# Two tiles of block two's first output projection as a pair with two groups of seven block products, and ScalarE's loop over pooled groups written out

## The reference, cut to what matters

```
hdn = rmsnorm(x, norm_a);  u, gate = hdn @ w_in_a          # two halves of 2048
z[:, g] = (pool_g(u[:, g]) @ w_grp_a[g]) * scale_a[g]      # g = 0..3, windows 2, 4, 8, 16
y = (z * silu(gate)) @ w_out_a;  x = x + y                 # "first output projection"
kv_in = rmsnorm(x, norm_kv);  k = rope(kv_in @ w_k);  v = kv_in @ w_v
```

## Time and profile before

| | us |
|---|---|
| median of 3 runs | 2318.03 (2317.78 to 2319.93) |
| profiled execution, its own time | 2317.87 |
| its span | 2316.1 |
| PE busy | 2299.1 (99%) |
| DVE busy | 1824.8 (79%) |
| ACT busy | 1185.2 (51%) |
| POOL busy | 449.1 (19%) |

### The profile page before, as it was taken

One profiled execution on the slowest core, in us unless ns is written; L12 is line 12 of the kernel. 1 busy time (PEld: TensorE's weight loads), 2 busy tenths in 40 slices (PEclk: granted clock), 3 DMA queues, 4 the chain that ended last, 5 costly groups with the idle time before them and its releaser, 6 DMA issues.

```text
span 2316.1 us, 31102 instructions
## 1 busy us (share of the span) xinstructions
PE 2299.1 (99%) x10665; PEld 1886.4 (81%) x10665; DVE 1824.8 (79%) x2349; ACT 1185.2 (51%) x1510; POOL 449.1 (19%) x878
## 2 busy tenths in 40 slices
PE   9999999999999999999999999999999999999998
PEld 6878788888878888888888888888888888888887
DVE  5888899999777676888688886666788768888764
ACT  3544546544574444555455565445655544444653
POOL 0001001334001211212100001112012145686310
PEclk9999999999999999999999999999999999999999
DMA  9996569999958887666666656666556676666564
GB/s 392 396 335 245 162 232 370 355 338 342 360 179 287 309 281 253 217 209 213 207 224 204 235 187 232 220 220 205 190 199 228 216 218 189 193 203 200 183 211 153
DMA packets 178821, 566.95 MB, mean 245 GB/s; under 512 B 30816, under 2 KB 35200, under 8 KB 178304
## 3 DMA queue, kind: packets, MB, share of 16 engines
q1 hardware_dynamic: 145584, 528.28, 66.4%
q0 software_dynamic: 27136, 23.91, 3.5%
q10 hardware_dynamic: 5968, 13.00, 1.6%
HBM read 537.01 MB, written 4.21 MB: 234 GB/s over the span
## 4 chain that ended last, share of the span: by engine, by line
PE 90%; DVE 4%; DMA 3%; issue 1%; ACT 1%; ACTq 0%; SPq 0%; DVEq 0%
PE acc L2903 25%; PE acc L2904 25%; PE acc L2910 25%; DMA raw<-in_wa_dram 2%; DVE lo L1701 1%; PE tb L3398 1%; PE tb L3405 1%; PE tb L3399 1%; PE acc L3405 1%; PE acc L3398 1%; PE acc L3399 1%; DMA start_raw<-in_wa_dram 1%; PE tb L3597 1%; DVE macc L1934 1%; PE tb L2990 1%
## 5 line engine op out<-in xcount | busy, mean ns | idle before, releaser
L897 ACT ACTIVATE hi<-raw 128x1024 fp32r<-128x1024 f32 (+2 forms) x808 | 825.2, 1031 | 768.5 <-PE acc L2910 428.0
L1701 DVE TENSOR_TENSOR lo<-raw,hi 128x1024 fp32r<-128x1024 f32 (+1 forms) x748 | 892.0, 1209 | 318.8 <-ACT hi L897 312.9
L2903 PE MATMUL acc<-hi,Hh 128*128 128x512 f32 x1816 | 714.0, 393 | 1.9 <-issue 1.5
L2904 PE MATMUL acc<-hi,Hl 128*128 128x512 f32 x1816 | 707.4, 390 | 0.0
L2910 PE MATMUL acc<-lo,Hh 128*128 128x512 f32 x1816 | 485.7, 389 | 0.0
L2903 PEld LDWEIGHTS acc<-hi,Hh 128*128 128x128 f32 x1816 | 341.0, 188 | 80.3 <-issue 8.2
L2910 PEld LDWEIGHTS acc<-lo,Hh 128*128 128x128 f32 x1816 | 340.9, 188 | 71.3
L2904 PEld LDWEIGHTS acc<-hi,Hl 128*128 128x128 f32 x1816 | 341.1, 188 | 69.2 <-issue 0.2
L2903 PE MATMUL acc<-hi,hbh 128*128 128x512 f32 x512 | 202.8, 396 | 0.0
L2904 PE MATMUL acc<-hi,hbl 128*128 128x512 f32 x512 | 199.6, 390 | 0.0
L803 POOL DMA_DIRECT2D tok<-sgt x176 | 85.9, 497 | 493.0 <-DVE sgt L1877 381.8
(11 more groups left out here) (496 smaller groups left out, 2917.5 us busy)
## 6 DMA issues: line engine op xcount, KB each, us to landing
raw<-in_wa_dram SPq DMA_DIRECT2D x680, 512.0 KB, 4.5
raw<-in_wb_dram SPq DMA_DIRECT2D x96, 512.0 KB, 4.5
late_raw<-in_wa_dram SPq DMA_DIRECT2D x90, 512.0 KB, 6.6
start_raw<-in_wa_dram SPq DMA_DIRECT2D x70, 512.0 KB, 7.8
raw<-in_wc_dram SPq DMA_DIRECT2D x64, 512.0 KB, 4.2
tok<-sgt POOLq DMA_DIRECT2D x416, 32.0 KB, 4.3
landed<-sgt POOLq DMA_DIRECT2D x192, 32.0 KB, 4.1
pt_landed<-att_parts POOLq DMA_DIRECT2D x192, 12.0 KB, 3.1
```

The costliest lines, as they stand in the source:

```text
L897: act.activation(hi[:, s, n], w, ACT.Copy).then_inc(hi_ready, 1)
L1701: dve.tensor_tensor(lo[:, s, 0:n], raw[:, r, 0:n], hi[:, s, 0:n].bitcast(F32), ALU.subtract)\
L2903: pe.matmul(dst(tt), a, hi[:, s, w], start=first[tt] and i == 0, stop=False, skip_group_check=shared)
L2904: pe.matmul(dst(tt), b, hi[:, s, w], start=False, stop=False, skip_group_check=shared)
```

## The change

- Tiles 0 and 1 of the projection are computed as a pair of 36 - 16 = 20 ring places in place of 16 units: twelve plain units, and two groups of seven at places 6 and 11, for units 0 and 1 (k tiles 0 to 3) of both tiles. Places 0 to 5 hold tile 0's units 2 and 3, tile 1's 2 and 3, tile 0's 4 and 5; place 10 tile 1's unit 4; 15 and 16 tile 0's 6 and 7; 17 to 19 tile 1's 5 to 7. Tiles 2 and 3 are left as they are. The weights are laid out in memory in the new order.
- The forms of zh/zl's k tiles 0 to 3 are made on VectorE between pooled groups 2 and 3 (`out_slices` is the sum of both parts), rounded on ScalarE after two units of group 3, and split on VectorE after four.
- VectorE gets `combine_out` (five additions) behind place 16's remainder and `add_to_first` behind place 19's; ScalarE gets `copy_shared` behind place 16's rounding. TensorE waits for the sums before place 17. The first tile's `y2_add` and `y2_out` now stand behind the splits of places up to 19, those of the second tile behind place 23's.
- ScalarE's loop over groups 1 to 3 is written out.
- Counters and buffers are extended: a fifth `block_sums`, forms and sums in memory that is free there.

```diff
-KV_TURNS = len(GATED) + 2
+OUT_A0 = KV_AT[0] - 2 * 16 - 4
+OUT_TURN = len(GATED) + 2
+OUT_FIRST = len(SEVEN_AT)
+OUT_SEVEN = {0: 6, 1: 11}
+OUT_PLACES = {0: (0, 2), 1: (0, 3), 2: (1, 2), 3: (1, 3), 4: (0, 4), 5: (0, 5), 10: (1, 4), 15: (0, 6), 16: (0, 7),
+              17: (1, 5), 18: (1, 6), 19: (1, 7)}
+SEVEN_AT += [OUT_A0 + at for at in OUT_SEVEN.values()]
+KV_TURNS = OUT_TURN + 1
...
             pooled_group(0, 8 + 4 - 9, before_turn=1)
-            with c.loop(act, 3, unit=20, raw=20, u_turned=2) as g:
-                pooled_group(g + 1, last=g * MOVED + MOVED)
+            for g in range(1, 4):
+                if g == 3:
+                    split(2)
+                    round_forms(FORM_TILES + 1)
+                pooled_group(g, 8 if g < 3 else 6, last=g * MOVED)
...
-            split(7)
+            split_to(OUT_A0 + 17)
+            copy_shared(out_shared, OUT_A0 + 14, TT * OUT_TURN)
+            split_to(OUT_A0 + 20)
             y2_out(0)
-            split(8)
+            split_to(OUT_A0 + 24)
             y2_out(1)
...
-            for g in range(1, 4):
-                pooled_group(g)
+            pooled_group(1)
+            pooled_group(2)
+            chain(dve.tensor_tensor(out_slices[:], zh[:, 0:4, :].bitcast(F32), zl[:, 0:4, :].bitcast(F32), ALU.add))
+            add_forms(lambda f: out_forms[:, f], out_block)
+            split(4)
+            split_forms(FORM_TILES + 1)
+            pooled_group(3, 8 - 4)
+
+            def combine_out():
+
+                dve.wait_ge(unit_used, RING + OUT_A0 + 15)
+                dve.wait_ge(shared_copied, OUT_TURN + 1)
+                chain(dve.tensor_tensor(out_outer[:, 0, :], tb[:, 1, :], out_shared[:], ALU.add))
+                dve.tensor_tensor(out_inner[:], tb[:, 2, :], out_outer[:, 0, :], ALU.add)
+                chain(dve.tensor_tensor(out_outer[:, 0, :], tb[:, 3, :], out_outer[:, 0, :], ALU.add))
+                chain(dve.tensor_tensor(out_outer[:, 1, :], tb[:, 3, :], out_inner[:], ALU.add))
+                for b in range(1, 4):
+                    dve.sem_inc(tb_free[b], 1)
+                dve.tensor_tensor(acc[:, 2:4, :], acc[:, 2:4, :], out_outer[:], ALU.add).then_inc(sums_added, 1)
...
-            split(7)
+            split_to(OUT_A0 + 17)
+            combine_out()
+            split_to(OUT_A0 + 20)
+            dve.wait_ge(unit_used, RING + OUT_A0 + 17)
+            add_to_first((out_shared[:], out_inner[:]))
+            dve.wait_ge(first_summed, TT * (OUT_TURN + 1))
             y2_add(0)
             turn_blocks(head_major, y2_blocks, 0)
-            split(8)
+            split_to(OUT_A0 + 24)
             y2_add(1)
             dve.wait_ge(y2_moved, MOVED)
             turn_blocks(head_major, y2_blocks, 1)
...
-            tile(zh, zl, 0, 8, before={0: lambda: pe.wait_ge(z_split, 2), 4: lambda: pe.wait_ge(z_split, 3), 6: split_now}, after={1: last_group})
-            tile(zh, zl, 1, 8)
+            first_tiles = [open_tile(0)]
+            pe.wait_ge(z_split, 2)
+            at = 0
+            while at < 20:
+                if at in OUT_SEVEN.values():
+                    j = list(OUT_SEVEN.values()).index(at)
+                    if j == 0:
+                        for b in range(4):
+                            fill(b)
+                        pe.wait_ge(form_split, FORM_TILES + 2)
+                    seven_products((tb[:, 0, :], tb[:, 3, :], tb[:, 1, :], tb[:, 2, :], acc[:, 0, :], acc[:, 2, :], acc[:, 1, :]),
+                                   lambda e, tt: (zh[:, 2 * j + e, halves[tt]], zl[:, 2 * j + e, halves[tt]]),
+                                   lambda f: (formh[FORM_TILES + 1][:, f, j, :], forml[FORM_TILES + 1][:, f, j, :]), j == 0, j == 1, joined=True)
+                    at += 4
+                    continue
+                t, i = OUT_PLACES[at]
+                if (t, i) == (1, 2):
+                    first_tiles.append(open_tile(1))
+                if (t, i) == (0, 4):
+                    pe.wait_ge(z_split, 3)
+                if (t, i) == (0, 6):
+                    split_now()
+                if (t, i) == (1, 5):
+                    pe.wait_ge(sums_added, OUT_TURN + 1)
+                unit(first_tiles[t], zh, zl, 2 * i, 2, N, i == 2, (t, i) in ((0, 7), (1, 4), (1, 7)), shared=t == 1)
+                if at == 1:
+                    last_group()
+                at += 1
```

More of the change, by code:

```diff
@@ L68 @@
 A_LOADS = 4 * 19 + 8 + 8 * 8 + 4 * 8 + 4 * 8 + FT * 16 + 4 * (FK // 2) + 4 * 20 + 3 * 32
-A_UNITS = A_LOADS + 2 * (2 * 8 + 2 * 4 + 2 * 3)
+A_UNITS = A_LOADS + 2 * (2 * 8 + 2 * 4 + 2 + 2 * 3)
 Q_HEADS = 4
@@ L388, in two_blocks @@
         h_forms = sb("h_forms", [P, FORMS, 2, P], at=x_at)
-        block_sums = [sb(f"block_sums{i}", [P, 2, UNIT], at=at) for i, at in enumerate((x_at, h_at + 8 * KB, tok_at, free + 64 * KB))]
+        block_sums = [sb(f"block_sums{i}", [P, 2, UNIT], at=at) for i, at in enumerate((x_at, h_at + 8 * KB, tok_at, free + 48 * KB, free + 64 * KB))]
         gated_outer = sb("gated_outer", [P, 2, N], at=free + 2 * FK * T * 4)
@@ L424, in two_blocks @@
         att2 = sb("att2", [P, NG * 384])
+        out_forms = sb("out_forms", [P, FORMS, 2, P], at=free + 32 * KB)
+        out_slices = sb("out_slices", [P, 4, T], at=free + 36 * KB)
+        out_outer = sb("out_outer", [P, 2, N], at=free + 56 * KB)
+        out_inner = sb("out_inner", [P, N], at=free + 60 * KB)
+        out_shared = sb("out_shared", [P, N], at=free + 62 * KB)
         kv_forms = sb("kv_forms", [P, FORMS, 2, P], at=att2_at)
@@ L427, in two_blocks @@
         formh, forml = ([sb(f"form{part}{i}", [P, FORMS, 2, P], F32R, at=at)[:] for i, at in enumerate(ats)] for part, ats in (
-            ("h", (x_at + 8 * KB, x_at, x_at + 8 * KB, h_at + 16 * KB, free + 72 * KB)),
-            ("l", (x_at + 12 * KB, x_at + 4 * KB, x_at + 12 * KB, h_at + 20 * KB, free + 76 * KB))))
+            ("h", (x_at + 8 * KB, x_at, x_at + 8 * KB, h_at + 16 * KB, free + 40 * KB, free + 72 * KB)),
+            ("l", (x_at + 12 * KB, x_at + 4 * KB, x_at + 12 * KB, h_at + 20 * KB, free + 44 * KB, free + 76 * KB))))
         for parts, hid in ((formh, hidh), (forml, hidl)):
@@ L587, in sums_of @@
         def sums_of(group):
-            return block_sums[0 if group < len(GATED_AT) else 1 if group < len(GATED_AT) + len(FORM_UNITS) else 2 if group < KV_FIRST else 3]
+            return block_sums[0 if group < len(GATED_AT) else 1 if group < len(GATED_AT) + len(FORM_UNITS) else 2 if group < OUT_FIRST else 3 if group < KV_FIRST else 4]
         def form_source(i):
-            return h_forms if i == 0 else forms if i <= FORM_TILES else kv_forms
+            return h_forms if i == 0 else forms if i <= FORM_TILES else out_forms if i == FORM_TILES + 1 else kv_forms
         def late_sums(block):
@@ L1544, in _ @@
             split_to(KV_AT[0] + 14)
-            round_forms(FORM_TILES + 1)
+            round_forms(FORM_TILES + 2)
             for i in range(4):
@@ L2638, in _, with out_block @@
             pooled_group(0, 8 + 4 - 9)
-            for g in range(1, 4):
-                pooled_group(g)
+            def out_block(tt, e):
+                return out_slices[:, :, tt * P:(tt + 1) * P].rearrange("p (j e) t -> p e j t", e=2)[:, e]
+            pooled_group(1)
[15 more added lines that the diff above has]
+                dve.tensor_tensor(acc[:, 2:4, :], acc[:, 2:4, :], out_outer[:], ALU.add).then_inc(sums_added, 1)
             split(1)
@@ L2726, in _ @@
                     split_to(at + 15)
-                    split_forms(FORM_TILES + 1)
+                    split_forms(FORM_TILES + 2)
                 split_to(KV_AT[n + 1] + 6)
@@ L3387, in _, with seven_products @@
             tile(Hh, Hl, 1, 8, before={0: lambda: pe.wait_ge(x_split, 7), 2: lambda: pe.wait_ge(x_split, 8)})
-            def seven_products(banks, plain, summed, first, last):
+            def seven_products(banks, plain, summed, first, last, joined=False):
                 x1, x5, x6, x7, c11, c12, c21 = banks
                 for part, groups in enumerate((((x1, plain(0, 0), 0, first, last), (c11, plain(1, 0), 1, False, False)),
-                                               ((c12, summed(3), 1, first, last),),
+                                               ((c12, summed(3), 1, first and not joined, last),),
                                                ((x5, summed(0), 0, first, last), (x7, summed(2), 1, first, last)),
@@ L3582, in _ @@
             for n in range(1, 4):
-                tiles_by_sevens(KV_PLAIN, KV_SEVEN, FORM_TILES + 1)
+                tiles_by_sevens(KV_PLAIN, KV_SEVEN, FORM_TILES + 2)
             def scores(head):
@@ L3739, in _layout @@
         wa += [_units(w_in_a[:, g * N:(g + 1) * N]), _units(w_in_a[:, D + g * N:D + (g + 1) * N]), grp]
-    wa += [_units(a["w_out_a_2"][0])]
+    out_a = by_tile(a["w_out_a_2"][0])
+    places = {place: out_a[t][i:i + 1] for place, (t, i) in OUT_PLACES.items()}
```

(2 more changed lines are left out.)

## The result

| kernel | median us | runs | lowest to highest | ratio to before, 95% interval |
|---|---|---|---|---|
| before | 2318.43 | 11 | 2317.70 to 2319.93 | |
| changed | 2323.79 | 11 | 2322.83 to 2326.86 | 1.0025 (1.0017 to 1.0033) |

The change makes the kernel 5.4 us slower, where 0.3 us faster was forecast; the range ended at 2320.4. The prediction had taken 4.6 us for about what cannot be told from none; with 11 runs each the interval is 1.9 us to either side, so the loss is clear of the noise. The profiled execution of the changed kernel took 2326.68 us, 2325.0 of it in the span.

The account below looks back on a forecast made before the run. TensorE's number of matmuls was taken to set the end. Gain -1.36 plus wait 1.04 plus 0 gave -0.32 us: 2317.55 from the profiled run, 2317.7 us as the median; range 2315.8 to 2320.4.

Parts of the forecast that it names:

- the range: Whole run: 2315.8 to 2320.4 us, from rival 1 (whole gain stays) less about 0.9 to rival 2's (late block transfer) far end.
- The gain: Projection's first two tiles: two groups of seven remove 6 matmuls at 0.2267 us each, 1.36 us.
- The forms: VectorE after pooled group 2: sums and forms delay the next remainder 2.7 us; cost nothing, with 1.8 us to spare.
- The sevens on VectorE: Projection: a group of seven takes VectorE 6.7 us against TensorE's 4.76; spaced as in the keys with more lead, cost nothing.
- The loop: ScalarE's loop over pooled groups written out: put at 0, ends minus and plus 0.2 us.
- The tb banks: Place 6: all four must be free, the last freed by z's last transposes, already waited for ahead of unit 6.
- t0: The end of the second group of seven on TensorE, from which the prediction counts its times.
- The sums: VectorE's combination behind the second seven: done at t0 + 5.19, TensorE waits from t0 + 5.44; fits by 0.25 us, costs nothing.
- The wait at unit 20: Third tile's first unit: rounding stands behind the first tile's copies and squares; TensorE waits 1.04 us, bounds 0 and 1.6.
- The block transfer: VectorE's wait for the first tile's transfer holds up unit 24's remainder: 0 to 0.7 us, taken as 0.
- Rival 4: The change doesn't reach the end as counted: forms or freed loop shift something by several us elsewhere; chance 0.07.
- The last sign on the list: A change over 2 us in either direction would mean that the cause is not in the prediction's account.

Follow-up runs that it names:

- e6: e5 with VectorE issuing the combination's last addition before it releases the tb banks; median 2317.23 us, 0.9995 of before.
- e1: The changed kernel without the wait for tb banks 0 and 1 ahead of tile 0's unit 6 (place 15); median 2321.31 us, 1.0010 of before.
- e2: The changed kernel, bank wait kept, with tb bank 1 released behind the combination's first addition in place of the fourth; median 2321.00 us, 1.0011 of before.
- e7: The changed kernel with tb banks 1 and 2 released behind the combination's third addition in place of the fourth; median 2322.93 us, 1.0020 of before.
- e4: e1 with ScalarE rounding units 20 and 21 before it copies and squares the first tile; median 2320.43 us, 1.0010 of before.
- e5: e4 with VectorE making the remainders of units 24 to 27 before it waits for the first tile's block transfer; median 2317.54 us, 0.9995 of before.

## Why the prediction was wrong

- **The gain** was right: 6 matmuls, 1.36 us, sevens at full pitch; e6's trace shows it whole.
- **The forms** were right: 2.82 us on VectorE (2.7 predicted), no wait. **The sevens on VectorE** too. **The loop**: nothing that can be told, as said.
- **The tb banks: this step failed.** It read "The four tb banks must be free at place 6; the last of them is freed by the remainders of z's last transposes, for which the kernel already waits ahead of its unit 6." That is the old meaning of `split_now`. The helper (the code behind this list) waits until tb banks 0 and 1 are released as often as the program has filled them so far, and the change moves it from unit 6, where the last fills were z's transposes, past a new fill of all four banks to place 15. There it asks for the release of this fill's bank 1, which VectorE gives behind its fourth addition. The z it once guarded had been waited for by the fill at place 6. Every number needed stood in the rows: VectorE's first addition ends at t0 + 0.89 + 0.68, the fourth at t0 + 0.89 + (1234.31 - 0.34 - 1231.24) = t0 + 3.6, TensorE is there at t0. Cost: 3.79 us of waiting, where the prediction had nothing. e1 takes it away, e2 and e7 move it.
- **The clock** was not thought of, since no gap was foreseen: 2.67 us more.
- **The sums** were mis-sized: t0 + 5.19 predicted, 5.6 in e4 and e5, because of 0.69 us between the last two additions where the down projection has 0.34. In the changed kernel it is hidden by the bank wait; in e1, e4 and e5 it costs 0.3, in e6 nothing. So the cover of 0.25 us that the prediction called thin was not there.
- **The wait at unit 20** was right in place, chain and size (e1: 1.13, e4: gone), and is not in the changed kernel: TensorE is 6.5 us later there, so ScalarE has the time.
- **The block transfer** was the right mechanism with too small a price: 0 to 0.7 us, 1.62 in e1. The landing came 13.5 us behind the first issue, and with that the prediction's own sum, from POOL's first issue to the remainder of unit 24 against TensorE's need for it, gives the wait (12.96 + 13.5 + 2.45 - 27.33 = 1.6). It had taken the median landing of one transfer, 3.7 us, but VectorE waits for the last to land, which took 5.3 in the kernel before and 6.2 in e1. What follows was left out: the weight ring refilled late, 1.24 us at the third tile and 0.41 in the keys. The changed kernel shows the last two in part (0.35 and 0.41).
- **The range** left out a wait of VectorE's whole combination, because the waits that the change moves were not recounted one by one. Rival 4 ("no row speaks for it") comes nearest to what happened, but the causes that it names, the forms and the loop, were not the ones. The last sign on the list held: a change over 2 us meant that the cause was not in the account.

The helpers on TensorE, and the wait as the changed kernel has it, cut to the lines that matter and with one comment added; `c.at` is the number of fills that the program has written so far, and the 1 stands for the first, free state:

```
def taken(*banks):
    for b in banks:
        pe.wait_ge(tb_free[b], c.at(f"tb{b}") + 1)
def fill(b):
    taken(b)
    c.up(f"tb{b}")
...
split_now = lambda: taken(0, 1)
...
if (t, i) == (0, 6):     # place 15, behind fill(0) to fill(3) at place 6
    split_now()
```

## What to carry to other kernels

A wait on a running count changes its meaning when it is moved past whatever raises the count: recompute the number for each wait that a reordering moves, before costing anything else. A wait that bites hides those behind it; take it away and look at what is late next, since here 2.7 us of relief came with the wait and 3.6 more only when two queue orders were mended as well (e5). When a tile's end is moved nearer to its next use, count in whole queues: what each engine does between the tile's end and the next unit, and whether it waits there for a transfer.

## What the runs showed of the hardware that was not expected

- TensorE idle for 3.63 us went on at half clock (0.427 us from start to start), idle for 2.91 us it fell to half after two more matmuls, idle for 1.58 us it went on at the full one, all three behind the same steady run of matmuls, each in one trace. The Trainium skill (TensorE: Matmul & The Clock Gate, part 1) gives 426.7 ns at N = 512 for the cold array; the trace agrees.
- A wait that only semaphore instructions end was "issue" in the profile of the changed kernel and of e7, with no releaser, and in e2 it was put down to an engine that had long been done. Its end against the other engines' last instructions (0.16 us behind VectorE's addition in all three) found the cause.
- Three semaphore increments between two dependent additions on VectorE: 0.69 us of idle time here, 0.34 in the down projection. With two (e2) it was 0.25 us, and with none (e6) the later addition started 0.65 us sooner than with three. Why three cost more here than in the down projection is open.
